# Splitting of out weights moved in two mixers, three waits, turned copies and a sum moved in a two-block transformer kernel

## The chip, the cores and the metric

The kernel runs as one launch on 1 core of a Trainium2 chip. The metric is device time in microseconds. Engines are named PE (TensorE), ACT (ScalarE), DVE (VectorE), POOL (GpSimd) and SP (SyncE, which issues most DMAs).

## The reference

512 positions, 1024 channels, float32. The first block has two layers, the second block one. Cut to what the change touches:

```python
# first block, each of two layers
h = rms_norm(x, attn_norm_w[layer]); proj = h @ w_in[layer]
o_a = hgrn2_mixer(...)       # gated linear recurrence, both directions, 256 channels
o_b = fourier_mixer(b_u)     # real part of the 2-D DFT over positions and 64 channels
o_c = dilated_attention_mixer(c_q, c_k, c_v, positions)     # 8 heads, rotary
x = x + concatenate([o_a, o_b, o_c]) @ w_out[layer]
h = rms_norm(x, mlp_norm_w[layer])
x = x + square(relu(h @ w_up[layer])) @ w_down[layer]
# second block
cols = rmsnorm(x, mix_norm_g) @ w_in
y_rw  = rwkv7_mix(...)       # matrix-state recurrence, 8 heads of 64
y_mla = mla_mix(...)         # causal latent attention
merged = gate_rw * (y_rw @ w_branch_rw) + gate_mla * (y_mla @ w_branch_mla)
x = x + merged @ w_out
h2 = rmsnorm(x, ffn_norm_g)
x = x + hier_moe(h2, ...)    # 4 groups of 8 experts; each token: top group, top 2 experts
out = rmsnorm(x, final_norm_g)
```

## The kernel before

**Layout and programs.** The activations lie turned, channels on partitions: X is 8 tiles of 128x512. A large product is done in three passes over operands split into a high and a low part (fp32r): high x high, low x high, high x low. ScalarE makes the high part of a weight unit of 128x1024 (WH, `act_hi`), VectorE the low part (WL, `dve_lo`); there are three unit buffers, and two slots of raw weights (`raw`) that SP fills chunk by chunk in a fixed order, each when the slot's last reader is done. A chunk is two units. `first_units` (line 748) makes both units of a layer's first chunk. Each engine has one program, a fixed list of instructions, and waits for semaphores where the data come from another engine.

**Order by weaving.** `weave` (line 205) steps through a string; each letter runs one engine's stream up to its next `yield`. The same string is used on all engines, so a bare `yield` in one stream shifts its later steps against the other streams on that engine alone. In the mixers (`MIX`, line 1429) u is the wide stream (projections, then the Fourier part, then the attention) and c the linear recurrence. The last letters are c u c: the last c is the recurrence's end (`rec_pe`: two 32-row products; `rec_dve`: four multiplications of 128x512, then two low parts; `rec_act`: two high parts), the u ahead of it the first half of the Fourier part (`four_pe`, `four_act`, `four_dve`, from line 1209). So ScalarE's order was: copies of half 0, high parts of the out weights, the recurrence's high parts, copies of half 1, high parts of the result. VectorE's: low parts of the out weights, the recurrence's four multiplications and two low parts, low parts of the result, attention. TensorE: product of half 0, the recurrence's two, product of half 1, four products that join the halves (constants cd and sd), attention (`att_pe`).

**Second block.** `RWKV` (line 1919) weaves c (the recurrence: `rw_pe`, `rw_act`, `rw_dve`), g (8 gate projections, 4 steps each) and b (products of the attention's branch), where `filled` puts g 33 times and then b 8 times for the letters f. At the entry `rw_dve` centres the decay sums (step 6), then multiplies four tensors of 128x2048 by exponentials (step 7; the second of them signals "first", for which TensorE's first scores wait), then masks the scores (step 8). Gate results lie in three PSUM banks in turn; a bank is free when VectorE has taken its result (`dve_made`).

**Merge.** At the recurrence's end `rw_dve` makes the output in four quarters ("gn", 0 to 3; three instructions each). `mrg_pe` (line 2126) multiplies by two chunks of w_branch_rw: eight results in four banks, each the sum of four 128-row products, all behind the wait for quarter 3. `mrg_dve` takes a result, gates it, adds the other branch, and makes the low part of the one before; `mrg_act` makes its high part. Then come the first units of w_out, and the out projection (`pe_lins`).

**Router and experts.** `mo_pe` (line 2231) multiplies logits, turns H into rows (32 transposes, 8 banks), then the rank product of one-hot matrices (waits for "mk" of VectorE), the count, and the list product (waits for P and R of VectorE). From the list VectorE makes indices, GpSimd gathers the rows of the first expert, TensorE turns them. In experts 2 to 9 TensorE also turns one half of a 128-token tile of X in four transposes of 128x128, and ScalarE copies it into Xr. PSUM banks go round in a cycle of eight (`Turn`), each reader calls `next` in the same order. Xr has the addresses of H. The expert loop fetches 3 MB of weights per expert, gathers up to 128 rows and scatters the results.

**Last sum.** For each tile of 128 tokens (0 to 3): VectorE adds the two expert results of a token (128x1024), adds Xr, ScalarE squares and takes the root, VectorE inverts and scales (line 2585).

## Time and profile before

| | us |
|---|---|
| median of 3 runs (2408.35 to 2412.47) | 2410.22 |
| the profiled execution | 2411.03 |
| its span | 2409.1 |
| PE busy (93%) | 2241.8 |
| DVE busy (55%) | 1315.3 |
| ACT busy (37%) | 897.5 |
| POOL busy (9%) | 212.4 |
| VectorE, addition or multiplication 128x512 | 0.69 |
| VectorE, 128x1024 with two operands in SBUF (R_moe group) | 1.22 |
| ScalarE, copy of 128x512 out of PSUM | 0.60 |
| raw weights of w_out, 1 MB, issue to landing (median) | 4.8 |

The page gives, per engine, the busy time; the chain that ended last, followed back from the last instruction; and the costliest groups. TensorE's matmuls overlap one another, so its busy share also covers time in which it doesn't run at its peak. A product of float32 operands stands as two records. The timeline shows neighbours of the same kind as one line with a count; in brackets is how long the engine had been idle, and which instruction of which engine ended that. PEclk is the granted clock of TensorE as a part of 2.4 GHz: 0.5 is 1.2 GHz.

### The profile page before, as it was taken

How to read it: one execution, taken by the hardware profiler on the slowest of the kernel's cores; microseconds unless marked ns; L12 is line 12 of the kernel's file. 1: busy time of each engine (PE TensorE's matmuls, PEld its weight loads, DVE VectorE, ACT ScalarE, POOL GpSimd, SP SyncE). 2: the span in 40 equal slices, each digit the busy share in tenths (PEclk: the TensorE clock that was granted, in tenths of full speed). 3: DMA queues.
4: the chain of work that ended last, by engine and by line, in shares of the span. 5: the costliest groups of instructions: out<-in, count | busy, mean ns of one | idle time of the engine just before them, and what ended most of it. 6: DMA issues, size and time to landing. Idle time of an engine off the chain costs nothing.

```text
span 2409.1 us, 33736 instructions
## 1 busy us (share of the span) xinstructions
PE 2241.8 (93%) x14488; PEld 1724.2 (72%) x14488; DVE 1315.3 (55%) x1929; ACT 897.5 (37%) x1327; POOL 212.4 (9%) x168
## 2 busy tenths in 40 slices
PE   6999899999999988899999998997999978999995
PEld 5778478888887875588888876565788647677773
DVE  6756555525536674656335454666433354677775
ACT  5422553312223322733223332344221123666663
POOL 1112000000010121010000110000000001222220
PEclk9999999999999999999999999999999988999997
DMA  4211112232322112022222221311111224689884
GB/s 157 71 52 37 53 36 101 91 105 88 105 88 88 53 53 70 1 88 88 105 90 103 94 86 38 114 49 66 63 55 60 83 87 187 237 323 354 342 332 191
DMA packets 51848, 270.21 MB, mean 112 GB/s; under 512 B 12144, under 2 KB 12272, under 8 KB 22512
## 3 DMA queue, kind: packets, MB, share of 16 engines
q1 hardware_dynamic: 41472, 256.67, 29.3%
q0 software_dynamic: 9216, 8.42, 1.0%
q10 hardware_dynamic: 1008, 2.92, 0.3%
q8 instruction: 116, 1.90, 0.3%
q14 instruction: 36, 0.29, 0.0%
HBM read 266.92 MB, written 26.21 MB: 122 GB/s over the span
## 4 chain that ended last, share of the span: by engine, by line
PE 83%; DVE 9%; ACT 4%; issue 2%; DMA 1%; POOL 0%; SPq 0%; DVEq 0%; POOLq 0%; ACTq 0%
PE psum L123 80%; PE psum L126 3%; DVE A_mix L136 2%; DVE A_second L136 1%; ACT A_mix L130 1%; DVE WL L136 1%; ACT WH L130 1%; DVE A_second L144 1%; DVE A_mix L156 1%; DVE A_moe L136 1%; ACT A_mix L133 1%; DMA raw<-in_w_in 0%; DVE A_mix L162 0%; DVE A_mix L153 0%; DVE A_second L150 0%
## 5 line engine op out<-in xcount | busy, mean ns | idle before, releaser
L136 DVE TENSOR_TENSOR WL<-raw,WH 128x1024 fp32r<-128x1024 f32 x236 | 298.6, 1267 | 421.8 <-ACT WH L130 421.5
L130 ACT ACTIVATE WH<-raw 128x1024 fp32r<-128x1024 f32 x236 | 248.3, 1054 | 431.1 <-PE psum L123 402.7
L123 PE MATMUL psum<-HH,WH 128*128 128x512 f32 x736 | 307.1, 417 | 46.3 <-DVE A_second L136 21.0
L123 PE MATMUL psum<-R_op,WH 128*128 128x512 f32 x1024 | 316.1, 390 | 0.0
L123 PE MATMUL psum<-R_ffn,WH 128*128 128x512 f32 x1024 | 315.3, 389 | 0.0
L123 PE MATMUL psum<-HL,WH 128*128 128x512 f32 x736 | 294.5, 400 | 0.0
L123 PE MATMUL psum<-HH,WL 128*128 128x512 f32 x736 | 294.3, 400 | 0.0
L123 PEld LDWEIGHTS psum<-R_op,WH 128*128 128x128 f32 x1024 | 192.2, 188 | 40.7 <-issue 1.0
L123 PEld LDWEIGHTS psum<-R_ffn,WH 128*128 128x128 f32 x1024 | 192.2, 188 | 39.8
L123 PEld LDWEIGHTS psum<-HH,WH 128*128 128x128 f32 x736 | 142.9, 194 | 93.9 <-issue 31.5
L123 PE MATMUL psum<-R_ffn,WL 128*128 128x512 f32 x512 | 199.2, 389 | 0.0
L123 PE MATMUL psum<-R_op,WL 128*128 128x512 f32 x512 | 199.2, 389 | 0.0
L123 PE MATMUL psum<-A_mix 64*128 64x64 f32 (+5 forms) x1984 | 165.8, 309 | 35.5 <-DVE A_mix L136 22.2
L136 DVE TENSOR_TENSOR R_moe<-ring_moe,R_moe 128x1024 fp32r<-128x1024 f32 x128 | 153.5, 1221 | 61.2 <-ACT R_moe L130 58.6
L123 PE MATMUL psum<-R_moe 128*128 128x512 f32 x768 | 184.8, 396 | 2.3 <-DVE R_moe L136 2.3
L123 PEld LDWEIGHTS psum<-A_mix 64*128 64x128 f32 (+2 forms) x1984 | 117.1, 173 | 73.5 <-issue 36.6
L123 PE MATMUL psum<-A_second 64*64 64x64 f32 (+4 forms) x3736 | 156.8, 235 | 12.9 <-ACT A_second L130 3.9
L123 PEld LDWEIGHTS psum<-R_moe 128*128 128x128 f32 x768 | 142.9, 189 | 31.7 <-ACT R_moe L130 1.9
L123 PEld LDWEIGHTS psum<-HH,WL 128*128 128x128 f32 x736 | 142.6, 194 | 31.5
L123 PEld LDWEIGHTS psum<-HL,WH 128*128 128x128 f32 x736 | 143.0, 194 | 30.6 <-issue 2.6
L130 ACT ACTIVATE R_moe<-ring_moe 128x1024 fp32r<-128x1024 f32 x128 | 135.6, 1061 | 53.2 <-PE psum L123 52.7
L123 PEld LDWEIGHTS psum<-A_second 64*64 64x64 f32 (+3 forms) x3736 | 126.2, 137 | 40.8 <-issue 25.9
(198 smaller groups left out, 2944.0 us busy)
## 6 DMA issues: line engine op xcount, KB each, us to landing
ring_moe<-in_w_gu SPq DMA_DIRECT2D x64, 1024.0 KB, 9.9
raw<-in_w_in SPq DMA_DIRECT2D x42, 1024.0 KB, 4.8
raw<-in_w_up SPq DMA_DIRECT2D x32, 1024.0 KB, 4.8
raw<-in_w_down SPq DMA_DIRECT2D x32, 1024.0 KB, 4.8
ring_moe<-in_w_dn SPq DMA_DIRECT2D x32, 1024.0 KB, 7.3
raw<-in_w_out SPq DMA_DIRECT2D x12, 1024.0 KB, 4.8
kept<-A_second SPq DMA_DIRECT2D x20, 256.0 KB, 2.1
raw<-in_dft SPq DMA_DIRECT2D x4, 1024.0 KB, 4.8
```

Source lines behind the costliest of these rows:

```text
L123: return self.raw.matmul(o, l, r, start=start, stop=stop)
L126: return self.raw.matmul(o, i, ident, is_transpose=True, start=True, stop=True)
L130: return self.raw.activation(o, i, f, scale=scale)
L133: return self.raw.activation(o, i, f, scale=scale, bias=bias, accum_out=accum)
L136: return self.raw.tensor_tensor(o, a, b, op)
L144: return self.raw.scalar_tensor_tensor(o, a, s, b, op0, op1)
L156: return self.raw.copy_predicated(o, m, a)
```

## The change

1. `four_act` and `four_dve`: the first units of the mixers' out weights are split in the second half's step, behind the recurrence's end and ahead of half 1's copies.
2. `rw_pe`, `rw_act`, `rw_dve` get one more `yield` each, and the string one more c and another order. On VectorE the four large multiplications are two and two in different steps, and four f stand ahead of them instead of two.
3. `mrg_pe` runs the first chunk by quarters of the output, into four banks at once, each quarter behind its own wait; results lie in eight banks. The first units of w_out are split within the merge (ScalarE behind its high part 5, VectorE ahead of result 7).
4. The 32 transposes of X and ScalarE's eight copies move from experts 2 to 9 into the router: 8 ahead of the rank product, 16 between count and list, 8 behind the list.
5. GpSimd adds the two expert results of tiles 2 and 3.

```diff
@@ -1211,11 +1211,11 @@
                     e.wait_ge(*at("rot_dve", ly, "a", 7))
+                else:
+                    first_units(e, x.out[0], act_hi)
...
                     e.act(x.us[part * 2 + d], bk(part * 2 + d), ACT.Copy).then_inc(*did("fou_act", ly, part, d))
-                if part == 0:
-                    first_units(e, x.out[0], act_hi)
@@ -1223,8 +1223,8 @@
         def four_dve(e, x):
+            yield
             first_units(e, x.out[0], dve_lo)
-            yield
@@ -1536,6 +1536,7 @@
                     yield
+            yield
@@ -1661,6 +1662,7 @@
             yield
+            yield
@@ -1797,6 +1799,7 @@
             e.tt(chunked(s2.aa), chunked(s2.aa), s2.E23[:, :, 1:65], MUL).then_inc(*did("rw_dve", "first"))
+            yield
@@ -1916,7 +1919,7 @@
         STATES = "cfccfcfccf"
-        RWKV = filled("cccfffcfcfcffcfff" + ("cfcfccfcfc" + STATES) * 2 + "cfcfcccfc" + STATES + "cccccc" + STATES + "cffcffc", g=33, b=8)
+        RWKV = filled("cccfffcfcfcffffcfc" + ("cfcfccfcfc" + STATES) * 2 + "cfcfcccfc" + STATES + "cccccc" + STATES + "cffcffc", g=33, b=8)
@@ -2104,7 +2107,7 @@
-        MB, RB = (0, 1, 2), (4, 5, 6, 7)
+        MB, RB = (0, 1, 2), tuple(range(8))
@@ -2127,16 +2130,29 @@
-            for n in s2.wr2_c:
-                run(wide_pe(e, n, s2.yrw, "r", RB, ready))
...
+            n = s2.wr2_c[0]
+            e.wait_ge(*at(f"raw{n % NRAW}", n))
+            e.wait_ge(*at("mrg_dve", "m", 7))
+            for kt in range(4):
+                e.wait_ge(*at("rw_dve", "gn", kt))
+                for m in range(4):
+                    t = e.mm(bk(RB[m]), slot(n)[:, kt * S + m * 128:kt * S + (m + 1) * 128], s2.yrw[:, kt, :], kt == 0, kt == 3)
+                    if kt == 3 and m < 3:
+                        t.then_inc(*did("mrg_pe", "r", m))
+            t.then_inc(*did("raw_use", n))
+            mark("raw_use", "r", 3)
+            run(wide_pe(e, s2.wr2_c[1], s2.yrw, "r", RB, ready))
...
             for i in range(9):
+                if i == 7:
+                    first_units(e, s2.out[0], dve_lo)
...
                     e.wait_ge(*wide_made("r", i))
-                    e.tt(tb, bk(RB[i % 4]), s2.gate[:, i, :], MUL).then_inc(*did("mrg_dve", "r", i))
+                    e.tt(tb, bk(RB[i]), s2.gate[:, i, :], MUL).then_inc(*did("mrg_dve", "r", i))
@@ -2148,6 +2164,9 @@
                 e.act(HHt[:, i, :], s2.tb[i % 4], ACT.Copy).then_inc(*did("mrg_act", "hi", i))
+                if i == 5:
+                    e.wait_ge(*wide_made("m", 7))
+                    first_units(e, s2.out[0], act_hi)
@@ -2252,6 +2271,16 @@
+            def turned_x(k):
...
+                for f2 in range(2):
+                    b = bank()
+                    for f in range(4):
+                        t = e.tr(b[:, f * 128:(f + 1) * 128], Xt[:, f2 * 4 + f, k * 128:(k + 1) * 128], ident)
+                    t.then_inc(*did("mo_pe", "xr", k, f2))
...
+            turned_x(0)
@@ -2262,6 +2291,8 @@
             t.then_inc(*did("mo_pe", "count"))
+            turned_x(1)
+            turned_x(2)
@@ -2270,6 +2301,7 @@
             t.then_inc(*did("mo_pe", "list"))
+            turned_x(3)
@@ -2312,12 +2344,6 @@
                     down(x - 1)
-                if 2 <= x < 10:
-                    k, f2 = divmod(x - 2, 2)
-                    b = bank()
-                    for f in range(4):
-                        t = e.tr(b[:, f * 128:(f + 1) * 128], Xt[:, f2 * 4 + f, k * 128:(k + 1) * 128], ident)
-                    t.then_inc(*did("mo_pe", "xr", k, f2))
@@ -2365,9 +2391,21 @@
+            def turned_x(k):
+                for f2 in range(2):
+                    n, b = turn.next()
+                    e.wait_ge(*at("mo_pe", "xr", k, f2))
+                    e.act(mo.Xr[k][:, f2 * S:(f2 + 1) * S], b, ACT.Copy).then_inc(*read("mo_act", turn, n))
+                    mark("mo_act", "xr", k, f2)
...
+            turned_x(0)
...
             turn.next()
+            turned_x(1)
+            turned_x(2)
             turn.next()
+            turned_x(3)
@@ -2402,12 +2440,6 @@
                     down(x - 1)
-                if 2 <= x < 10:
-                    k, f2 = divmod(x - 2, 2)
-                    n, b = turn.next()
-                    e.wait_ge(*at("mo_pe", "xr", k, f2))
-                    e.act(mo.Xr[k][:, f2 * S:(f2 + 1) * S], b, ACT.Copy).then_inc(*read("mo_act", turn, n))
-                    mark("mo_act", "xr", k, f2)
@@ -2447,6 +2479,10 @@
             ov_pool(e)
+            for k in (2, 3):
+                y = mo.Y2[k][:, 0:D]
+                e.wait_ge(*at(f"Y{k}"))
+                e.tt(y, y, mo.Y2[k][:, D:2 * D], ADD).then_inc(*did("mo_pool", "ys", k))
@@ -2483,7 +2519,7 @@
             e.wait_ge(*last("mo_dve"))
-            for _ in range(9):
+            for _ in range(1 + 8 + 2):
@@ -2521,6 +2557,8 @@
             e.cp(mo.cnt, b[:, 0:32]).then_inc(*read("mo_dve", turn, n))
+            for _ in range(4):
+                turn.next()
@@ -2530,6 +2568,8 @@
             mark("mo_dve", "gsl")
+            turn.next()
+            turn.next()
@@ -2576,8 +2616,6 @@
                     down(x - 1)
-                if 2 <= x < 10:
-                    turn.next()
@@ -2585,8 +2623,11 @@
                     y = mo.Y2[k][:, 0:D]
-                    e.wait_ge(*at(f"Y{k}"))
-                    step(e.tt(y, y, mo.Y2[k][:, D:2 * D], ADD), "y", "sum", k)
+                    if k < 2:
+                        e.wait_ge(*at(f"Y{k}"))
+                        step(e.tt(y, y, mo.Y2[k][:, D:2 * D], ADD), "y", "sum", k)
+                    else:
+                        e.wait_ge(*at("mo_pool", "ys", k))
@@ -2814,8 +2855,6 @@
             mrg_act(e)
-            e.wait_ge(*wide_made("m", 7))
-            first_units(e, s2.out[0], act_hi)
@@ -2866,7 +2905,6 @@
             mrg_dve(e)
-            first_units(e, s2.out[0], dve_lo)
```

## Rows read from the trace of the kernel before

**Rows 1.** The page's chain that ended last: shares of the span by engine.
```profile
PE 83%; DVE 9%; ACT 4%; issue 2%; DMA 1%; POOL 0%; SPq 0%; DVEq 0%; POOLq 0%; ACTq 0%
```

**Rows 2.** Timeline, Fourier, layer 0: start us, us, engine line op out<-in xcount [idle before <-releaser].
```profile
255.03 7.13 PE L123 MATMUL psum<-raw,A_mix 128*128 128x512 f32 x16
...
258.82 2.00 ACT L130 ACTIVATE WH<-raw 128x1024 fp32r<-128x1024 f32 x2 [4.15 <-DMA raw<-in_w_out]
...
266.12 5.20 PE L123 MATMUL psum<-A_mix,C 128*128 128x512 f32 x8 [3.96 <-ACT A_mix L130]
...
272.59 0.68 DVE L162 CUSTOM_DVE_ANT_0 A_mix<-psum,C 128x512 f32<-128x512 f32 x1
```

**Rows 3.** Timeline, Fourier part, layer 1.
```profile
948.27 7.13 PE L123 MATMUL psum<-raw,A_mix 128*128 128x512 f32 x16
...
967.42 0.68 DVE L162 CUSTOM_DVE_ANT_0 A_mix<-psum,C 128x512 f32<-128x512 f32 x1
```

**Rows 4.** Chain that ended last: start us, us, what; both attentions become steady.
```profile
283.67 2.08 PE psum L123 x20
...
976.38 2.08 PE psum L123 x20
```

**Rows 5.** Windows, TensorE, layer 0's ramp: us, PE busy (x), PEclk, DMA share, GB/s.
```profile
276.00:279.00 3.00, 2.53 (x7) 0.50 0.00 0
```

**Rows 6.** Timeline, entry to the recurrence.
```profile
1680.94 8.89 DVE L136 TENSOR_TENSOR A_second<-A_second 128x2048 f32<-128x2048 f32 x4
...
1690.41 1.29 DVE L136 TENSOR_TENSOR A_second<-psum,RS 128x512 f32<-128x512 f32 x2
...
1691.16 0.79 PE L123 MATMUL psum<-HH,WH 128*128 128x512 f32 x1 [9.48 <-DVE A_second L136]
...
1696.31 2.08 PE L123 MATMUL psum<-A_second 64*64 64x64 f32 x64
...
1698.11 1.33 DVE L156 COPY_PREDICATED A_second<-M,psum 128x512 f32<-128x512 uint8 x2
```

**Rows 7.** Timeline, merge of the two branches and first out product.
```profile
1929.53 0.75 DVE L144 SCALAR_TENSOR_TENSOR A_second<-A_second,V,psum 128x512 f32<-128x512 f32 x1 [0.36 <-PE psum L123]
...
1938.44 29.32 PE L123 MATMUL psum<-A_second,raw 128*128 128x512 f32 x64 [8.94 <-DVE A_second L136]
...
1972.14 0.58 PE L123 MATMUL psum<-HH,WH 128*128 128x512 f32 x1 [4.38 <-DVE WL L136]
```

**Rows 8.** Windows, TensorE, router.
```profile
2026.00:2030.00 4.00, 4.00 (x26) 0.63 0.00 0
...
2030.00:2034.00 4.00, 2.24 (x18) 0.93 0.64 262
```

**Rows 9.** Timeline, TensorE, router.
```profile
2033.43 5.77 PE L123 MATMUL psum<-A_moe,C 128*128 128x32 f32 x28 [1.76 <-DVE A_moe L136]
...
2039.41 3.70 PE L123 MATMUL psum<-A_moe 128*128 128x96 f32 x16 [0.20 <-DVE A_moe L136]
```

**Rows 10.** Chain that ended last, expert loop, with and without copies of X.
```profile
2144.94 0.66 PE psum L126 x6
...
2165.86 0.22 PE psum L126 x2
...
2175.87 0.22 PE psum L126 x2
```

**Rows 11.** Windows: PE, PEld, DVE, ACT, POOL busy (x), PEclk, DMA share, GB/s.
```profile
2200.00:2300.00 100.00, 100.00 (x422) 70.16 (x421) 74.17 (x90) 66.58 (x90) 25.89 (x21) 1.00 0.90 344
```

**Rows 12.** Timeline, GpSimd and VectorE side by side.
```profile
222.84 3.40 POOL L136 TENSOR_TENSOR A_mix<-A_mix 128x1024 f32<-128x1024 f32 x1
...
224.50 2.28 DVE L136 TENSOR_TENSOR A_mix<-A_mix 128x512 f32<-128x512 f32 x1
```

**Rows 13.** Timeline, last sum.
```profile
2393.03 2.48 DVE L136 TENSOR_TENSOR A_moe<-A_moe 128x1024 f32<-128x1024 f32 x2 [0.81 <-DMA A_moe<-y_rows]
...
2404.83 1.28 DVE L144 SCALAR_TENSOR_TENSOR A_moe<-A_moe,raw 128x1024 f32<-128x1024 f32 x1
```

## The prediction

> **What bounds the kernel now.** I read the chain of waits first, by engine [rows 1]: TensorE's matmuls make 83% of it. So most of the span is TensorE working, and only two things shorten it: a stretch where TensorE stands idle waiting for another engine, or TensorE work moved into such a stretch. Next I read, by windows, where TensorE is under full busy time or at half clock, and then the timeline of each place that the diff touches: the Fourier part of both mixers [rows 2, 3] and the ramp behind it [rows 4, 5], the entry to the recurrence of the second block [rows 6], the merge of its two branches [rows 7], the router [rows 8, 9], the expert loop [rows 10, 11] and the last sum [rows 12, 13]. Behind each of the first three places stands a long stretch of TensorE work without gaps, so what a place gives there reaches the end. Times are from the profiled execution, which took 2411.03 us for a span of 2409.1; the median of the runs shown is 2410.22, so the profile stands 0.8 us above it. I sum against 2411.0.
>
> **Fourier part, twice.** In layer 0 the second product with the transform's table runs from 255.03 to 262.16. Its copies on ScalarE come only just before 266.1, because ScalarE, in order, first splits the out weights (waits for their DMA until 258.82, ends 260.82) and then waits for the recurrence's gated output, which VectorE delivers late: VectorE itself stood at the low part of that same split (its wait ends with ScalarE's half) [rows 2]. TensorE idles 3.96 us, falls to half clock, and the first row minimum of the attention comes at 272.59. After the change the recurrence's output (four VectorE steps of about 0.7) starts at about 254.7, when its two matmuls are done, and is through by 258.9. The split keeps its time, since the DMA sets it. The first copy, us[2], is done at 261.4 and us[3], which needs the end of the product, at 262.85. TensorE goes on at 262.2: four products of 0.855 (two records of 0.43 each at full clock) end at 265.6. Copy and low part (0.6 and 0.69, table) and the row minimum follow: 265.7 + 0.6 + 0.65 = 266.95, against 272.59: 5.6 us. Layer 1 by the same steps: product's end 955.4, plus 3.4 for the four products, plus 1.4 = 960.2, against 967.42: 7.2 us [rows 3].
> The ramp of the attention from its first row minimum to the steady pattern takes 11.1 us in layer 0 and 9.0 in layer 1 (283.67 and 976.38 less 272.59 and 967.42) [rows 2 to 4]. In layer 0 the clock falls to 0.50 again there [rows 5], in layer 1 it does not. With the gap gone TensorE enters both ramps busy, as much as it is in layer 1 now, so I take 9.0 for both: 2.1 us more in layer 0. Sum: 7.7 + 7.2 = 14.9; bounds 10.8 (both ramps with one half-clock stretch) and 15.
>
> **Three waits.** The strings of the weave move nothing on TensorE: its new yield is empty, and five gate steps stand before the first scores in both orders. On VectorE two gate steps now stand ahead of the big products. Before: four products 1680.94 to 1689.8, then the emptying of a gate bank at 1690.41; TensorE, which wants that bank, idles 9.48 us and runs the step at half clock (12 records to 1696.3) [rows 6]. After: the bank is emptied at 1681.05 to 1681.75, TensorE runs the step without a stop, to 1684.5. But ScalarE's sigmoid and split and VectorE's low part follow (from 1690.41 to 1694.5 in the rows, 4.1 us), and only then the first two products (half of 8.8 and a bit: 4.45): the scores can start at 1681.05 + 4.1 + 4.45 = 1689.6. The other two products and small copies take 4.95: 1694.5, then copies and mask 0.7, and the masks as now (1.94 from the first mask to the last): 1697.15. TensorE meanwhile has scores and one gate step (about 2.1 + 2.7, slower by up to 3 at half clock: ends by 1697.2). It goes on with the doubling steps at about 1697.2, against 1698.4 + 12 x 0.227 = 1701.0 before. Gain 3.8, not 9.5: the gap moves behind the gate step. Bounds 2 and 4.5.
>
> **Merge.** The four quarters of the recurrence's output come from VectorE between 1929.53 and 1938.4, one per 2.2 us; TensorE waits for the last (8.94 idle) and then does 64 records in 29.32, of which 1.9 is half clock (64 x 0.4275 = 27.4) [rows 7]. Now the first weight chunk goes by quarters into eight banks: start at 1931.8, each quarter 16 products/4 = 3.42 us, longer than 2.2, so no later wait: end 1959.2. Against 1938.44 + 29.32 = 1967.76 before, that is 8.5 earlier. The bank waits fall too: VectorE has 8 x 2.05 us of merging from 1943 on; it keeps up by the last piece. The out weights were split after the merge, and TensorE began the out projection at 1972.14, 4.38 idle behind VectorE's low part. Now the slot of the first chunk is free at 1945.5 (all four outputs of it end together), its DMA of 4.8 (table) lands at 1950.3, ScalarE splits at 1954.7 behind the sixth high part, VectorE's low part at 1957.9 to 1960.2; its first half (1959.1) is ready when TensorE comes (1959.2). The last low part comes at about 1962.9, needed at 1964.7. So the out projection starts 12.9 earlier. It began at half clock (at 0.43 a record, [rows 7] show the first with 0.58, instead of the 0.227 of the steady stream, for eight or nine records), which a TensorE without a gap does not: 1.7 more. Against that the 2.3 us gap at 1929.5 that stays may halve the clock for a while as now (0.8, a chance of a half times 1.7). Gain 13.8; bounds 9 and 14.7.
>
> **Router.** The 32 turned copies of X leave the experts: 0.66 against 0.22 us per expert, eight times 0.44 = 3.5 saved [rows 10]. In the router 8 fill the gap of 1.76 before the rank product; 8 lie beneath the gather of the rows, for which TensorE waits idle behind the list product; 16 stand ahead of the list product, which VectorE releases at about 2039.2, right when the count ends [rows 9]. These have no cover if the clock stays low: 16 x 0.143 = 2.3, less 0.2 of slack: 2.1 late. (0.143: seven a microsecond; at full clock nine.) If the first eight keep the clock up, rank and count (28 records at 0.206, half clock) shorten by up to half, the copies end at 2038.5, and the list gains until VectorE's own two low parts of weights in between (1.22 each by the table) hold it: 1.7 early. I take 0 for the list and 0.3 for a warmer first expert. Their ScalarE copies (8 x 0.6) run while it has nothing else until the gather. Gain 3.8, bounds 1.4 and 7.
> The windows show 26 records of which most are copies at 0.63, and 0.93 right behind them: the clock rose while TensorE did nothing but turn [rows 8].
> The Trainium skill, "TensorE: Matmul & The Clock Gate", Part 4 (PE-mode transpose), says that full clock does not engage for transposes, which do not count as busy work. By it the copies cannot hold the clock up, and the sum is 2.4 us higher. This trace goes against it.
>
> **Last sum.** GpSimd takes the first additions of tiles 2 and 3, off VectorE. A 128x1024 addition there takes 2.4 (3.40 with a wait of 1.1). And VectorE's addition issued at 224.50 takes 2.28 instead of 0.69: it ends 0.55 after GpSimd's end at 226.24. The two don't share, they exclude each other while both read two operands from SBUF [rows 12]. Serial from 2393.03: two VectorE additions (2.4), GpSimd 2.3, output 0 1.2, GpSimd 2.3, then addition, output, addition, output (4.8), root and last output 1.9: 2407.9, against 2406.1 [rows 13]. Cost 1.8; without the exclusion it would gain 2.3 (two additions off the path, less 0.1).
> The Trainium skill, "SBUF — State Buffer", section "Who interferes with whom", says that a VectorE instruction with two SBUF inputs contends with a GpSimd one that reads SBUF, and the later one fully blocks. The trace agrees (2.28 for 0.69). This rule speaks against this part of the change.
>
> **Sum.** 14.9 + 3.8 + 13.8 + 3.8 - 1.8 = 34.5. 2411.0 - 34.5 = 2376.5 us.
>
> **Rivals.**
> *Clock.* Each gap that stays can halve the clock for one stretch more: 2.1 in each attention ramp, 1.7 at the merge, 2.1 at the list. For it: layer 0's ramp does so now [rows 5]. Against: layer 1's does not. All four: 2376.5 + 8 = 2384.5.
> *Copies don't hold the clock.* The router's list comes 2.1 later and the first expert is as now: 2378.9. For it: the clock is at half through the rank product now. Against: the 0.93 behind the copies.
> *No exclusion in the last sum.* If tiles 2 and 3 land so that GpSimd works while VectorE waits: 2376.5 - 4.1 = 2372.4. Against: VectorE has no idle time after 2393.03.
> *VectorE bounds the merge.* Four results end within 2.6 us and want 2.05 each, and 2.4 of weight split is added. If the last low parts come over 1.8 later than TensorE wants them, TensorE stops before the second half of the first out unit, and half clock comes back: 13.8 shrinks to 7, 2383. Against: my count leaves 1.8 us.
> *Slower.* The expert loop turns transfer-bound: starting it with another phase makes each of 32 experts wait for its weights. An expert lasts 10.01 us without copies [rows 10]; the loop has to take over 34.5/32 = 1.1 more each before the whole is slower. At 1.3 more: 2376.5 + 41.6 = 2418. For it: the DMA engines are busy 0.90 in that loop [rows 11]. Against: the loop waits for none now, and that pace is already run by the last 22 experts.
>
> **How the numbers follow.** Forecast 60% (own range 2371 to 2381), clock 17%, copies 8%, no exclusion 10%, merge 4%, slower 1%. Range 2369 to 2387: low end with the router and the ramps at their good bounds and no exclusion, high end with the clock rival and some. 0.2% (4.8 us), what a measurement here tells from no change, is far inside the gain: faster 0.98, same 0.01, slower 0.01.
>
> **What would show it.** Row minimum directly behind the four products in both mixers, no gap over 1 us there; a TensorE gap of about 5 us behind the gate step, before the scores; out projection within 0.5 us of the merge's last product; no copies of X in the expert loop and the list product within 2 us of its old distance from the rank; in the last sum VectorE additions of about 3 us beside GpSimd's. Wrong would be: a wait for the out weights in the merge, or a first expert that begins over 4 us later after the rank product than now.

## Result and the profile after

The changed kernel takes 2382.27 us (median of 4 executions, 2381.16 to 2383.54) against 2411.34 for the kernel before (4, 2408.35 to 2413.39): ratio 0.9875, 95% interval 0.9863 to 0.9887 (the ratios here are estimated from all executions; the quotient of these two medians is 0.9879). That is 29.1 us less; the forecast was 34.5 less, 2376.5. The profiled execution took 2381.16 us, 29.9 under that of before, with a span of 2379.4. Two repetitions on other chips gave 0.9863 (0.9848 to 0.9878) and 0.9868 (0.9851 to 0.9886). All 13 executions of the changed kernel have a median of 2381.6 (2378.6 to 2388.1), all 33 of the kernel before, in the four groups of executions, 2413.1 (2408.0 to 2421.2): 31.5 us.

The chain of waits of the changed kernel still has TensorE as most of it [rows 1]:

```profile
PE 83%; DVE 9%; ACT 5%; issue 2%; DMA 1%; POOL 0%; SPq 0%; DVEq 0%; POOLq 0%; ACTq 0%
```

The Fourier part of layer 0, all engines in order of time (start, duration, engine, what it does):

```profile
254.89 0.69 DVE L136 TENSOR_TENSOR A_mix<-A_mix 128x512 f32<-128x512 f32 x1
...
256.53 2.00 ACT L130 ACTIVATE WH<-raw 128x1024 fp32r<-128x1024 f32 x2 [0.29 <-DMA raw<-in_w_out]
257.62 2.36 DVE L136 TENSOR_TENSOR WL<-raw,WH 128x1024 fp32r<-128x1024 f32 x2 [0.65 <-ACT WH L130]
258.44 0.58 ACT L130 ACTIVATE A_mix<-psum 128x512 f32<-128x512 f32 x1
259.64 3.60 PE L123 MATMUL psum<-A_mix,C 128*128 128x512 f32 x8
...
264.52 0.68 DVE L162 CUSTOM_DVE_ANT_0 A_mix<-psum,C 128x512 f32<-128x512 f32 x1
```

The recurrence's output is multiplied by its gate ahead of the split, the copies of the product follow it at once, and the joining products start at 259.64 without a gap. The 3.96 us of [rows 2] are gone. From the start of the second product (252.67) to the row minimum it takes 11.85 us instead of 17.56. The first product, which no edit touches, took 8.80 here and 7.10 before: it ran in part at half clock.

Behind it, TensorE in the attention ramp of layer 0. The gaps are the normal waits for the row minimum, and the third pair of scores takes 2.08 instead of 1.13, which is half clock (1.2 of 2.4 GHz, a granted clock of 0.50 in the views):

```profile
263.17 1.13 PE L123 MATMUL psum<-A_mix 64*128 64x512 f32 x4
265.87 1.13 PE L123 MATMUL psum<-A_mix 64*128 64x512 f32 x4 [1.57 <-DVE small L162]
268.40 2.08 PE L123 MATMUL psum<-A_mix 64*128 64x512 f32 x4 [1.40 <-DVE small L162]
```

TensorE at the entry to the recurrence [rows 6] and in the merge [rows 7], changed kernel:

```profile
1679.95 3.68 PE L123 MATMUL psum<-A_second 64*64 64x64 f32 x64 [4.86 <-DVE A_second L136]
1687.55 3.95 PE L123 MATMUL psum<-A_second 64*64 64x64 f32 x128 [0.64 <-DVE A_second L156]
...
1917.50 27.70 PE L123 MATMUL psum<-A_second,raw 128*128 128x512 f32 x64 [2.42 <-DVE A_second L136]
1945.02 0.50 PE L123 MATMUL psum<-HH,WH 128*128 128x512 f32 x1
```

The 9.48 us ahead of the gate step have become 4.86 behind it. What this is worth shows between two fixed points of TensorE's work, the gate step behind a wait of 2.9, which both kernels have, and the first doubling product. Before:

```profile
1669.14 0.79 PE L123 MATMUL psum<-HH,WH 128*128 128x512 f32 x1 [2.86 <-DVE A_second L136]
...
1701.26 3.95 PE L123 MATMUL psum<-A_second 64*64 64x64 f32 x128
```

That is 32.1 us. In the changed kernel it is 28.0 (1659.53 to 1687.55), 4.1 less. In the merge 8.94 have become 2.42, and the out projection follows the last product without any wait.

TensorE in the router and the first experts of the changed kernel [rows 9], and below it windows of the same stretch (busy time and records of PE, PEld, DVE, ACT and POOL, then the granted clock, DMA share and GB/s):

```profile
2002.76 1.04 PE L126 MATMUL psum<-C,X 128*128 128x128 f32 x8
2004.69 3.28 PE L123 MATMUL psum<-A_moe,C 128*128 128x32 f32 x28 [0.89 <-DVE A_moe L136]
2007.81 1.95 PE L126 MATMUL psum<-C,X 128*128 128x128 f32 x16
2009.59 1.92 PE L123 MATMUL psum<-A_moe 128*128 128x96 f32 x16
2011.35 1.04 PE L126 MATMUL psum<-C,X 128*128 128x128 f32 x8
2017.68 1.97 PE L126 MATMUL psum<-C,A_moe 128*128 128x128 f32 x8 [5.30 <-DMA A_moe<-h_rows,A_moe]
2021.15 7.77 PE L123 MATMUL psum<-R_moe 128*128 128x512 f32 x24 [1.50 <-DVE R_moe L136]
...
2032.69 7.21 PE L123 MATMUL psum<-R_moe 128*128 128x512 f32 x24 [0.85 <-ACT A_moe L130]
```

```profile
2003.00:2009.00 6.00, 5.11 (x47) 4.90 (x46) 5.38 (x23) 4.63 (x11) 0.00 (x0) 1.00 0.79 293
2009.00:2015.00 6.00, 3.38 (x31) 3.14 (x29) 5.58 (x20) 2.63 (x6) 1.35 (x2) 1.00 0.70 233
2015.00:2020.00 5.00, 1.97 (x8) 1.57 (x8) 0.47 (x1) 0.91 (x2) 1.84 (x2) 0.54 0.60 214
2020.00:2025.00 5.00, 3.85 (x9) 3.10 (x10) 0.92 (x2) 1.14 (x2) 0.98 (x1) 0.50 0.17 47
```

Rank and count take 3.28 us at full clock (5.77 before), the list 1.92 (3.70 before). TensorE then waits 5.30 us for the gathered rows, and behind the wait the clock is at half for the first expert: 7.77 us for the 24 records that took 7.08 before, and 7.21 in expert 1 where before had 5.74.

The last sum of the changed kernel, all engines; VectorE's operations beside GpSimd's take 3.4 instead of 1.2 or 1.3 [rows 13]:

```profile
2364.05 5.62 POOL L136 TENSOR_TENSOR A_moe<-A_moe 128x1024 f32<-128x1024 f32 x2 [13.28 <-DMA A_moe<-y_rows]
2364.10 3.38 DVE L144 SCALAR_TENSOR_TENSOR A_moe<-A_moe,raw 128x1024 f32<-128x1024 f32 x1
...
2367.40 3.36 DVE L136 TENSOR_TENSOR A_moe<-A_moe 128x1024 f32<-128x1024 f32 x1
```

### The profile page after: what moved, and what is told of

Read it like the earlier page. It is cut to its first block, busy times and chain, and to the rows that moved or that the text cites. A ratio compares the mean times of both kernels' runs of the same rounds, so it can differ in the third digit from the quotient of the medians.

```text
span 2379.4 us, 33737 instructions
## 1 busy us (share of the span) xinstructions
PE 2231.5 (94%) x14488; PEld 1716.7 (72%) x14488; DVE 1316.7 (55%) x1927; ACT 898.2 (38%) x1327; POOL 214.4 (9%) x170
## 4 chain that ended last, share of the span: by engine, by line
PE 83%; DVE 9%; ACT 5%; issue 2%; DMA 1%; POOL 0%; SPq 0%; DVEq 0%; POOLq 0%; ACTq 0%
PE psum L123 80%; PE psum L126 3%; DVE A_mix L136 2%; DVE A_second L136 1%; ACT A_mix L130 1%; DVE A_mix L156 1%; ACT WH L130 1%; DVE WL L136 1%; DVE A_second L144 1%; ACT A_mix L133 1%; DMA raw<-in_w_in 0%; DVE A_mix L162 0%; DVE A_mix L153 0%; ACT A_second L130 0%; DVE A_second L150 0%
```

## The experiments

Four groups of kernels ran (the first is the result above), each group on one chip beside the kernel before; ratios are to that. The theory: each part of the change does what its term says, and what is missing from the 34.5 us went to half clock, in stretches of TensorE's work that no edit touches. The rivals: a part gives less than its own stage shows, or the missing time lies in the unchanged stages because they now begin 8 us earlier.

### The last sum undone

```diff
-            for k in (2, 3):
-                y = mo.Y2[k][:, 0:D]
-                e.wait_ge(*at(f"Y{k}"))
-                e.tt(y, y, mo.Y2[k][:, D:2 * D], ADD).then_inc(*did("mo_pool", "ys", k))
...
-                    if k < 2:
-                        e.wait_ge(*at(f"Y{k}"))
-                        step(e.tt(y, y, mo.Y2[k][:, D:2 * D], ADD), "y", "sum", k)
-                    else:
-                        e.wait_ge(*at("mo_pool", "ys", k))
+                    e.wait_ge(*at(f"Y{k}"))
+                    step(e.tt(y, y, mo.Y2[k][:, D:2 * D], ADD), "y", "sum", k)
```

> The changed kernel with the last sum as before: VectorE does all four first additions, GpSimd none. Exclusion (VectorE and GpSimd can't both read two operands from SBUF): 1.8 us faster than the changed kernel, which stood at 2382.3, so 2380.5; the last 25 us have VectorE additions of 1.2 each and nothing of 3. No exclusion, GpSimd's two additions were a relief: 2.3 us slower, 2384.6.

Measured: 2375.02, ratio 0.9836 (0.9821 to 0.9851). The trace has 24.27 us from the first load of y_rows to the end, against 26.00 in the changed kernel and 24.23 before: 1.73, the price that was forecast. The median lies 7 us under the changed kernel's, more than that, so it was run again.

> The kernel with the last sum as before once more. Its trace showed 1.8 us less in the last sum and nothing else, but four of its five executions stood at 2373.7 to 2375.4, some 7 us under the changed kernel's. If 1.8 is the price of GpSimd's two additions and the rest is where the half-clock stretches fell: here 2378 to 2381, 1 to 3 us under the changed kernel of this group. If the last sum costs 7 (something at the start or in the instruction streams, outside the last sum): 2375 again.

Measured: 2379.45, 0.9865 (0.9850 to 0.9880), against 2380.29 for the changed kernel in the same group; last sum 24.24. Over both groups its nine executions have a median of 2377.7 and spread from 2373.7 to 2383.6. So 1.8 is the price by the traces, and 3.9 by all medians (2377.7 against 2381.6); the 7 us of the first group did not come back, and why four of its executions stood so close together at 2374 is open (their granted clock was 0.974 to 0.977, the profiled one's 0.973).

### All four additions on GpSimd

```diff
-            for k in (2, 3):
+            for k in range(4):
                 y = mo.Y2[k][:, 0:D]
                 e.wait_ge(*at(f"Y{k}"))
...
+                    e.wait_ge(*at("mo_pool", "ys", k))
```

> The changed kernel with all four first additions of the last sum on GpSimd instead of two. Exclusion: each addition that leaves VectorE costs 2.3 instead of 1.2 and takes VectorE's place for that time; two more make the last sum 2 to 2.5 longer, from the first load of y_rows to the end some 28 us instead of 26.0, and VectorE's additions and outputs beside them last 3 and more. No exclusion: VectorE has 1.2 less to do per tile, and the last sum ends with the last load plus 7: 24 or less.

Measured: 2384.19, 0.9879 (0.9864 to 0.9894), 3.9 over the changed kernel of its group; last sum 27.15 us. The direction and the long VectorE operations are those of the exclusion, but by the traces two more additions cost 1.15, not 2 to 2.5. GpSimd and VectorE in its last sum:

```profile
2359.28 2.33 POOL L136 TENSOR_TENSOR A_moe<-A_moe 128x1024 f32<-128x1024 f32 x1 [7.47 <-DMA A_moe<-y_rows]
2361.72 1.22 DVE L136 TENSOR_TENSOR A_moe<-A_moe 128x1024 f32<-128x1024 f32 x1 [11.72 <-POOL A_moe L136]
2362.53 8.20 POOL L136 TENSOR_TENSOR A_moe<-A_moe 128x1024 f32<-128x1024 f32 x3 [0.91 <-DMA A_moe<-y_rows]
2365.18 3.35 DVE L136 TENSOR_TENSOR A_moe<-A_moe 128x1024 f32<-128x1024 f32 x1 [2.23 <-POOL A_moe L136]
```

The first addition (2.33 for 1.22) ends before the second tile's load has landed: GpSimd itself then waits 0.91 for it. So its extra time costs little.

### The router's copies back in the experts

The change's part 4 undone, on TensorE (the same on ScalarE):

```diff
-            turned_x(0)
             b = bank()
             e.wait_ge(*at("mo_dve", "mk"))
...
-            turned_x(1)
-            turned_x(2)
...
+                if 2 <= x < 10:
+                    k, f2 = divmod(x - 2, 2)
+                    b = bank()
+                    for f in range(4):
+                        t = e.tr(b[:, f * 128:(f + 1) * 128], Xt[:, f2 * 4 + f, k * 128:(k + 1) * 128], ident)
+                    t.then_inc(*did("mo_pe", "xr", k, f2))
```

> The changed kernel with the turned copies of X back in experts 2 to 9. By my count and the two traces 3.5 us come back in the experts (eight times 0.44) and 1.4 in the router, because rank, count and list run at the half clock again (28 records in 5.8 instead of 3.3): 2387.2, and the granted clock stays 0.50 from the rows' turning to the first expert. If the copies don't hold the clock (what kept it in the changed kernel was the time of its start): rank and count keep about 3.3 us and only 3.5 comes back, 2385.8, or less, since the copies before the list product go away.

Measured: 2385.65, 0.9883 (0.9865 to 0.9900), 4.0 over the 2381.6 of all executions of the changed kernel. Its TensorE rows:

```profile
2003.90 5.70 PE L123 MATMUL psum<-A_moe,C 128*128 128x32 f32 x28 [1.76 <-DVE A_moe L136]
2009.81 3.70 PE L123 MATMUL psum<-A_moe 128*128 128x96 f32 x16 [0.20 <-DVE A_moe L136]
```

Half clock is back in rank, count and list, and from the turning of the rows to the first expert it takes 24.8 us instead of 23.6. The experts got 3.57 us longer (from expert 2 to the loop's last record 299.29 for 295.72), which is the eight copies (8 times 0.44 is 3.5). But experts 0 and 1 took 21.0 instead of 23.0: what the router gives, they took back. The clock of rank and count can be read in every trace: their 28 records take 3.2 to 3.8 us in all twelve with the copies beside them, and 5.77 and 5.70 in the two without.

### Empty work in the gaps

36 more turnings beneath the gather, into the bank that the last copies overwrite, and ten in each of the first two gaps of the attention ramp, into a bank that is not yet in use:

```diff
             turned_x(2)
...
-            turned_x(3)
+            turned_x(3, 36)
...
             score(0)
             for p in range(19):
+                if p < 2 and ly in (0, 1):
+                    for f in range(10):
+                        e.tr(bk(7)[:, f % 4 * 128:(f % 4 + 1) * 128], c("cd"), ident)
```

> The changed kernel with empty work for TensorE in gaps: 36 more turnings into the last bank of copies beneath the gather of the first expert's rows, and 10 in each of the first two gaps of the attention ramp of both mixers. If the clock is what the missing 4 to 5 us of the forecast went to: the turning of the gathered rows takes 1.0 instead of 2.0, expert 0's 24 records 5.7 instead of 7.8, the ramp of layer 0 goes from 11.0 to 9, that of layer 1 stays as it is: 4 to 5 us faster than the changed kernel, about 2377.5. If turnings don't hold the clock, or the gaps' lengths are set elsewhere: no gain, 2382.3, or up to 1 us slower by what sticks out.

Measured: 2378.03, 0.9845 (0.9830 to 0.9860). Expert 0 to expert 2 took 19.5 us instead of 23.0, the ramp of layer 0 10.98 instead of 13.00, that of layer 1 stayed at 10.98. That is 5.5 us by these stages, and 3.6 by the medians against all 13 executions of the changed kernel (no changed kernel ran in this group, and the interval reaches up to 0.9860, those of the changed kernel begin at 0.9848). Elsewhere the same trace lost 1.7 to half clock in the merge (M 54.9 in the table below).

### The Fourier part undone

```diff
                 if part == 0:
                     e.wait_ge(*at("rot_dve", ly, "a", 7))
-                else:
-                    first_units(e, x.out[0], act_hi)
                 for d in range(2):
...
+                if part == 0:
+                    first_units(e, x.out[0], act_hi)
...
         def four_dve(e, x):
-            yield
             first_units(e, x.out[0], dve_lo)
             yield
+            yield
```

> The changed kernel with the Fourier part of both mixers as before. The steps measured 5.7 us in layer 0 and 7.3 in layer 1, so by them alone 2382.3 + 13.0 = 2395.3. Theory of the unchanged stage: layer 1's mixers took 174.4 us before and 180.4 after, with the same instructions, because they began 8 us earlier and the half-clock stretches fell elsewhere; here they begin again when they began before, so they take 174.4 again and the whole is 2391.5 or less. If that stage's length has nothing to do with where it begins: 2395.3, with 180 us in it.

Measured: 2394.58, 0.9915 (0.9899 to 0.9931): 13.0 over the 2381.6, as the steps say, but from six executions that spread from 2390.3 to 2398.8. The theory of the earlier start fell. On TensorE the trace runs with that of before to 0.07 us up to 760 us, well behind the attention of layer 0, and then the stretch from there to layer 1's Fourier part takes 481.80 us, not 475.75. The same instructions at the same times came out 6 us apart. Where a half-clock stretch falls is not fixed by the program's own times.

### The changed kernel again, twice

> The changed kernel itself once more, beside the others of this group, to see how far one kernel differs from execution to execution. If where the half-clock stretches fall is fixed by the program's own times, every landmark of its trace lies within 0.3 us of the first one, the mixers of layer 1 take 180.4 us again and expert 0 to expert 2 23.0. If it changes from one execution to the next (the kernel with the old Fourier part began layer 1 where the kernel before did, and its mixers took 180.4 instead of 174.4): the same stages come out with either value, 174 to 182 and 19.5 to 23, and single times spread over 5 us or more.

> The changed kernel a third time, as the yardstick of this group on its chip: 2380 to 2385 by its eight executions so far (2379.9 to 2385.6), with the half-clock stretches in other places again.

Measured: 2381.61 (2379.87 to 2385.60) and 2380.29 (2378.57 to 2388.11). The out projection, an unbroken stream of TensorE work, by windows. First the changed kernel as first profiled, then its second execution, fifty microseconds each:

```profile
1945.02:1995.02 50.00, 50.00 (x251) 42.44 (x250) 16.88 (x19) 17.19 (x24) 7.72 (x6) 1.00 0.51 198
```

```profile
1946.90:1996.90 50.00, 50.00 (x237) 42.03 (x236) 16.91 (x19) 15.61 (x22) 7.72 (x6) 0.97 0.49 192
```

TensorE is busy for all of both windows, and the second one's clock was 0.97. The loss lies in four of its microseconds, where TensorE did 12 records of 128x512 (some 17 at full clock, at 0.227 each):

```profile
1985.11 3.65 PE L123 MATMUL psum<-raw,A_moe 128*128 128x36 f32 x32
```

```profile
1989.00:1993.00 4.00, 4.00 (x12) 3.15 (x11) 0.00 (x0) 0.00 (x0) 0.00 (x0) 0.57 0.00 0
```

TensorE had no gap there, but its work was not all alike: the clock fell right behind 32 narrow records of 36 columns, and the same holds in the trace of the last sum undone (records from 1984.43, 0.51 granted over 1988.5 to 1991.9). The first trace has these records too (1983.23) and stays at full clock.

The first product of layer 0's Fourier part differs in the same way, behind an equal wait. First profile, then the second:

```profile
242.88 8.80 PE L123 MATMUL psum<-raw,A_mix 128*128 128x512 f32 x16 [2.32 <-ACT A_mix L130]
```

```profile
246.69 7.11 PE L123 MATMUL psum<-raw,A_mix 128*128 128x512 f32 x16 [2.31 <-ACT A_mix L130]
```

The table has the stages of all traces, from the start of one landmark to the start of the next, in us. F0 and F1: Fourier part, first product to row minimum; A0 and A1: attention ramp, up to a landmark 2.0 later than the prediction's (so 13.0 is its 11.0); L: from the second half of layer 0's FFN to the Fourier part of layer 1; W: second block's attention to the recurrence's end (holds the three waits); M: from there to the out projection; O: out projection to the turning of the rows; G: from there to expert 0; X: expert 0 to 2; E: expert 2 to the loop's end; S: last sum.

| trace | F0 | A0 | L | F1 | A1 | W | M | O | G | X | E | S |
|---|---|---|---|---|---|---|---|---|---|---|---|---|
| before | 25.7 | 13.1 | 475.8 | 27.2 | 11.0 | 365.2 | 65.9 | 54.2 | 25.1 | 20.8 | 299.3 | 24.2 |
| changed | 21.6 | 13.0 | 481.8 | 19.9 | 11.0 | 360.7 | 53.2 | 52.6 | 23.6 | 23.0 | 295.7 | 26.0 |
| changed, second | 19.9 | 11.0 | 477.1 | 21.6 | 13.0 | 361.5 | 54.8 | 55.6 | 22.9 | 23.3 | 295.7 | 26.0 |
| changed, third | 21.6 | 13.0 | 481.8 | 19.9 | 12.8 | 361.8 | 53.2 | 52.6 | 23.6 | 23.3 | 295.7 | 26.0 |
| last sum undone | 21.6 | 13.0 | 481.9 | 19.9 | 11.0 | 361.5 | 53.2 | 55.7 | 23.3 | 22.8 | 295.7 | 24.3 |
| the same again | 19.9 | 11.0 | 477.2 | 21.6 | 13.1 | 362.4 | 53.2 | 52.6 | 23.0 | 23.3 | 295.7 | 24.2 |
| copies in experts | 21.6 | 13.0 | 481.8 | 19.9 | 11.0 | 360.7 | 53.2 | 52.6 | 24.8 | 21.0 | 299.3 | 26.0 |
| Fourier undone | 25.6 | 13.1 | 481.8 | 25.9 | 11.9 | 363.7 | 53.2 | 54.6 | 23.5 | 20.8 | 295.7 | 25.8 |
| waits undone | 19.9 | 12.8 | 478.8 | 21.6 | 11.9 | 365.1 | 54.9 | 54.2 | 23.3 | 22.6 | 295.7 | 25.7 |
| merge undone | 21.6 | 13.1 | 481.8 | 19.9 | 11.0 | 360.4 | 65.8 | 54.2 | 22.9 | 23.4 | 295.5 | 25.9 |
| four on GpSimd | 19.9 | 11.0 | 477.1 | 21.6 | 13.0 | 362.6 | 53.2 | 52.6 | 23.1 | 23.2 | 295.7 | 27.2 |
| filled | 19.9 | 11.0 | 477.1 | 21.6 | 11.0 | 362.6 | 54.9 | 54.3 | 23.1 | 19.5 | 295.7 | 26.1 |
| filled, all | 21.6 | 11.0 | 480.2 | 19.9 | 11.0 | 362.4 | 54.9 | 52.6 | 22.8 | 19.5 | 295.7 | 23.9 |
| filled, no last sum | 19.9 | 11.0 | 477.1 | 21.6 | 11.0 | 362.8 | 54.9 | 54.4 | 24.7 | 20.8 | 295.7 | 24.3 |

Stages without an edit have two or three lengths in one and the same kernel (L 477.1 and 481.8, O 52.6 and 55.6, A1 11.0 and 13.0), and which of them comes does not follow the edits. The stretch ahead of the table is such a stage too: the first product of F0 starts at 246.9 before, at 242.9 in the changed kernel, and at 242.1 to 246.9 over all traces, with no edit ahead of it.

The lengths are not independent of each other. In each of the twelve traces with the new Fourier part exactly one of F0 and F1 is 21.6 and the other 19.9, the first product being the difference. In the nine of them without filling, L is 481.8 or 481.9 where it is F0 (five traces) and 477.1 to 478.8 where it is F1 (four). And the ramp goes with the first product ahead of it: behind 21.6 it was long in eight of nine cases (the ninth 11.9), behind 19.9 short in seven of nine. What sets the pattern is open.

### The three waits undone

The three added `yield` lines out and the old string back:

```diff
-        RWKV = filled("cccfffcfcfcffffcfc" + ("cfcfccfcfc" + STATES) * 2 + "cfcfcccfc" + STATES + "cccccc" + STATES + "cffcffc", g=33, b=8)
+        RWKV = filled("cccfffcfcfcffcfff" + ("cfcfccfcfc" + STATES) * 2 + "cfcfcccfc" + STATES + "cccccc" + STATES + "cffcffc", g=33, b=8)
```

> The changed kernel with the three waits as before. By the stage's length 4.1 us slower than the changed kernel: TensorE waits some 9 us before the gate step at the entry of the recurrence instead of 5 behind it, and runs that step at half clock. If the gain in that stage was an accident of the clock and not of the order: within 1 us of the changed kernel, with the long wait back and something else shorter.

Measured: 2387.19, 0.9897 (0.9880 to 0.9914), 5.6 over the changed kernel of its group, whose interval reaches from 0.9848 to 0.9878. The stage W is 365.1, as before, and TensorE stands before the gate step again, and runs it at half clock (a record every 0.43 us in place of 0.23):

```profile
1680.49 0.80 PE L123 MATMUL psum<-HH,WH 128*128 128x512 f32 x1 [9.24 <-DVE A_second L136]
```

Between the two fixed points of above (1658.47 to 1691.22) it takes 32.8 us. In all twelve traces with the waits it takes 28.0.

### The merge undone

The banks, the loop over chunks and the place of the split as before:

```diff
-        MB, RB = (0, 1, 2), tuple(range(8))
+        MB, RB = (0, 1, 2), (4, 5, 6, 7)
...
-                if i == 7:
-                    first_units(e, s2.out[0], dve_lo)
...
+            e.wait_ge(*wide_made("m", 7))
+            first_units(e, s2.out[0], act_hi)
             run(act_lins(e, s2.out))
```

> The changed kernel with the merge of the two branches as before. The stage from the recurrence's last product to the out projection was 12.7 us shorter after the change, and the first 26 records of the out projection are at full clock by it: 12.7 to 14.4 slower than the changed kernel, 2395.0 to 2396.7. If the eight banks and the earlier split only moved the wait (TensorE is fast in the merge and then stands before the out weights): under 9.

Measured: 2394.51, 0.9918 (0.9905 to 0.9932): 12.9 over the changed kernel of its group. Both waits are back:

```profile
1924.38 29.17 PE L123 MATMUL psum<-A_second,raw 128*128 128x512 f32 x64 [8.94 <-DVE A_second L136]
1957.93 0.70 PE L123 MATMUL psum<-HH,WH 128*128 128x512 f32 x1 [4.38 <-DVE WL L136]
```

### Filled, with the last sum as before

The edits of the filled kernel and of the last sum together, and in the first of the two kernels a third filling:

```diff
+            ahead = [bank()]
+            for f in range(34):
+                e.tr(ahead[0][:, f % 4 * 128:(f % 4 + 1) * 128], c("cd"), ident)
             e.wait_ge(*at("rw_dve", "first"))
```

> The changed kernel with the last sum as before, the turnings of the filled kernel beneath the gather and in the attention ramps, and 34 more turnings for TensorE where it waits about 5 us before the recurrence's first scores. 1.8 us from the last sum and 4 from the fillings already measured; the scores ran from 1677 to 1684 at half clock, and if TensorE sets that stage up to 2 us more: 7 to 8 us faster than the changed kernel. If VectorE sets the stage behind the scores, the third filling gives nothing: 5 to 6 us. If fillings only trade one half-clock stretch for another, 2.

> The changed kernel with the last sum as before and the two fillings that gained (beneath the gather, and in the attention ramps), without the one before the recurrence's scores, which the trace showed to gain nothing (VectorE ends that stage) and to have a half-clock stretch of 1.5 us behind it. 1.8 + 3.5 to 4 under the changed kernel of this group; if the third filling was worth something after all, 3 or less.

Measured: 2376.83, 0.9847 (0.9833 to 0.9860) with the third filling, against 2381.61 for the changed kernel beside it; 2377.04, 0.9848 (0.9834 to 0.9861) without, against 2380.29. Ten executions of the two have a median of 2376.9, 4.7 under the 13 of the changed kernel. But both kernels also have the last sum undone: against the nine executions with that edit alone (2377.7) the fillings are worth 0.8, and 2.4 in the one group that has both (2377.04 and 2379.45). TensorE in the kernel with all three fillings, at the gather:

```profile
2010.92 4.97 PE L126 MATMUL psum<-C,X 128*128 128x128 f32 x44
2017.14 1.09 PE L126 MATMUL psum<-C,A_moe 128*128 128x128 f32 x8 [1.25 <-DMA A_moe<-h_rows,A_moe]
2019.97 5.74 PE L123 MATMUL psum<-R_moe 128*128 128x512 f32 x24 [1.73 <-DVE R_moe L136]
...
2029.45 5.73 PE L123 MATMUL psum<-R_moe 128*128 128x512 f32 x24 [0.85 <-ACT A_moe L130]
```

Both experts run at full clock. The same kernel at the recurrence's scores:

```profile
1676.08 2.08 PE L123 MATMUL psum<-A_second 64*64 64x64 f32 x64 [1.16 <-DVE A_second L136]
1683.67 5.50 PE L123 MATMUL psum<-A_second 64*64 64x64 f32 x128 [2.52 <-DVE A_second L156]
```

The scores take 2.08 instead of 3.68, but TensorE then waits 2.52 for VectorE instead of 0.64, and the next records fell to half clock (5.50 for 3.95). The doubling starts 28.0 us behind the fixed point as in the others. The third filling gives nothing.

## Why the prediction was right, point by point

**The whole.** The forecast of 2376.5 was 5.8 us too low: 2382.3 lies in the stated range (2369 to 2387), but outside the range that the forecast called its own (2371 to 2381, at 60%), and nearer to the clock rival's 2384.5 (at 17%). Over all executions the gain of 31.5 would put it inside. The mechanism of each part came as described; what the sum lacks is half clock.

**Fourier part, 14.9.** Right in its steps: 5.71 and 7.3 by the first trace (5.64 and 7.2 forecast), 13.0 by undoing it. From the second product to the row minimum all twelve traces with the new order have 11.8, the two with the old one 17.6 in layer 0, and 19.2 and 17.8 in layer 1. So 1.4 of layer 1's gain was half clock of one trace (its joining products took 6.67 there, 5.38 where the part was undone), which the forecast took for a property of the kernel. The 2.1 for layer 0's ramp is the term that failed: "With the gap gone TensorE enters both ramps busy, so I take 9.0 for both". Three of the nine traces that have this part and no filling show the short ramp, six the long one, and layer 1 has the long one in four of the same nine. TensorE entered all of them without the 4 us gap, so that gap's absence does not decide it; the first product ahead goes with it, as above. Nor did the forecast price that product: in one of the two layers it takes 1.7 more, in every trace with the new order. A filled ramp was short in six cases out of six.

**Three waits, 3.8.** Between the two fixed points it takes 28.0 us in all twelve traces with the waits and 32.1 and 32.8 in the two without: 4.1 to 4.7. The whole stage W, with more half clock in it than that, is 360.4 to 363.7 with the waits and 365.1 and 365.2 without; 5.6 by the medians. The gap moved behind the gate step and measured 4.86, as said ("about 5").

**Merge, 13.8.** 12.7 from the recurrence's end to the out projection (12.9 forecast), and no half clock at the out projection's start, 1.6 more (O 52.6 for 54.2). The chance that was priced at 0.8 came out so: five of the twelve traces with the new merge had 1.6 to 1.7 us of half clock in it (M 54.8 or 54.9 instead of 53.2). 12.9 by undoing it.

**Router, 3.8.** The 3.5 of the experts came out as 3.6. The list, forecast at 0, began 1.1 us earlier behind the rank (4.90 instead of 5.98) and was itself 1.8 shorter, all at full clock. Of that 1.5 reached the first expert (G 23.6 for 25.1). The list's earlier start is not what counts: in eight of the other eleven traces with the copies it began 6.0 to 7.1 behind the rank, and the unfilled ones among all twelve still have G at 22.9 to 23.6. The term "0.3 for a warmer first expert" has the wrong sign: experts 0 and 1 take 22.6 to 23.4 instead of 20.8 in eight of the nine traces with the copies moved and no filling. From the rows' turning to expert 2 the two orders are equal (45.9 and 45.8 with the copies in the experts; 45.9 to 46.9 moved, once 44.3). Whether the later clock loss follows from the earlier gain, the runs don't settle; the two traces with copies in the experts are few.

The copies did hold the clock, which the rival denied: granted 1.00 over 2003 to 2015, with 32 copies among the work, and in the filled kernel 44 turnings in a row at 0.11 us each, with the expert behind them at full clock (5.70 to 5.74 in the three traces that have the 44, where nine others have 7.1 to 8.1 behind the wait). They don't always hold it: see the last window of this document. The Trainium skill, "TensorE: Matmul & The Clock Gate", Part 4 (PE-mode transpose), which says that full clock does not engage for transposes, is not what these fp32 turnings show.

**Last sum, cost 1.8.** 1.73 to 1.77 in the traces. The Trainium skill, "SBUF — State Buffer", section "Who interferes with whom", names the block of the later one; 3.38 for 1.28 agrees. For four additions my count was too high (1.15 for two more, 2 expected), since it left out that some of them fall into waits for loads.

**The sum.** The parts undone one by one cost 13.0 + 5.6 + 12.9 + 4.0 and give back 3.9 by medians (1.8 by the traces): 31.6, against 31.5 measured over all executions and 34.5 forecast. That the two agree to 0.1 is luck: each part is a difference of medians of 4 to 13 executions, the intervals of the ratios reach 3 to 4 us to either side, and with the traces' 1.8 it is 33.7.

The stages say more. Between the first two traces (29.7 us of span) the edited stages gave 5.7 + 7.3 (Fourier), 0.1 (ramps), 4.1 (waits), 12.7 + 1.6 (merge, start of the out projection), 1.5 - 2.2 + 3.6 (router, experts 0 and 1, loop) and -1.8 (last sum): 32.6. Against the 34.5 the ramp is 2.0 short and the router 0.9, and the others are 1.0 over. The remaining 2.9 were lost where nothing was edited: 4.0 won ahead of layer 0's Fourier part, 1.7 lost in its first product, 6.1 lost between the ramp of layer 0 and layer 1's Fourier part, 0.9 won elsewhere. The traces of one kernel swing by as much from execution to execution (242.1 to 246.7 ahead of the Fourier part, 477.1 to 481.8 in L, in the changed kernel's own three).

The trace of before that all sums start from was itself a good one: 2411.0 where the 33 executions have a median of 2413.1, with L at 475.8, which no other trace reached. So the first pair of profiles shows 1.6 us less gain than the medians over all.

**Rivals.** The clock rival (2384.5) came nearest, in part by luck. Of its four places layer 0's ramp stayed long in the first trace, the other ramp, the merge and the list did not lose; its 8 counts 0.8 of the merge that the sum has already. And it priced the edited gaps alone, while the largest swings (L, O) lie where nothing was edited. Copies that don't hold the clock would have left rank and count at 5.8 us (3.28); without the exclusion the last sum would have been shorter, not 1.8 longer; VectorE did not stop TensorE in the merge (no wait before the out projection); the expert loop did not slow (295.7 us, 3.6 less).

## What to carry to other kernels

A gap of TensorE costs its length and then, in some executions, 1.6 to 2.3 us of half clock behind it: in five of twelve traces at the merge, in ten of eighteen at the unfilled ramps, in eight of nine at the first experts. Put that into the sum as a mean, and don't book a clock gain for one gap while others stay near it. Work without a use, placed where TensorE waits for something else anyway, brought G and X together from 45.9 to 46.9 (once 44.3) down to 42.3 and 42.5 in two traces and 45.5 in the third; by the medians of whole executions it gave 0.8 to 3.6, which lies within the intervals. It gives nothing where another engine ends the stage. When a change is worth less than 5 us of 2400, compare the stage it touches in two traces, not the totals, and look at the same stage in more than one execution of each kernel.

## What the hardware showed that was not expected

The changed kernel differs from execution to execution by up to 9.5 us, within one group, and the granted clock goes with it in the main: 0.974 in the shortest (2378.57) and 0.969 in the longest (2388.11). Stretches at half clock come also where TensorE is busy without a gap, as in the out projection above behind narrow products, where three lengths of one stage were seen (52.6, 54.2 to 54.6, 55.6).

In the last filled kernel the clock was at half while TensorE was busy with copies and the list product; ahead of that stood a wait of 1.18 and the rank's 28 narrow records (3.82 us). The window, same columns as above, shows 6.00 of 6.00 busy at 0.54:

```profile
2009.00:2015.00 6.00, 6.00 (x32) 6.00 (x32) 5.40 (x13) 2.73 (x5) 0.00 (x0) 0.54 0.74 276
```

So the fillings do not guarantee full clock. Over the whole run it was 0.974 to 0.979 in the 15 executions of the filled kernels and 0.969 to 0.976 in the 13 of the changed one, but four executions without filling (the last sum undone) had 0.974 to 0.977 as well.
